# Output projections in three places: VectorE's order around the gates, and the sum of two gated branches moved from GpSimd to VectorE

## The reference

```python
# block one
y = sigmoid(g_a) * (o_a @ w_pa) + sigmoid(g_b) * (o_b @ w_pb)
out = y @ w_out
# each of the two layers
projected = einsum('bsnw,nwd->bsnd', branches, w_branch[l])     # three branches of width 512
merged = sum(gates * projected, axis=branch)
h = h + einsum('bsd,de->bse', merged, w_out[l])
```

## Time and profile before

| | us |
|---|---|
| median of 3 runs | 1981.39 (1981.3 to 1981.52) |
| the profiled execution, its own time | 1982.14 |
| its span in the trace | 1980.4 |
| TensorE busy | 1890.6 |
| VectorE busy | 1128.7 |
| GpSimd busy | 592.2 |
| ScalarE busy | 357.5 |

### The profile page before, as it was taken

The page is one execution under the profiler, slowest core; times in us unless marked ns, Lnnn a source line. Parts: engine busy times, 40 slices in busy tenths (PEclk is TensorE's granted clock), DMA queues, the critical chain, the costliest instruction groups (busy, mean ns, idle before and its releaser), DMA issues.

```text
span 1980.4 us, 32402 instructions
## 1 busy us (share of the span) xinstructions
PE 1890.6 (95%) x13598; PEld 1731.1 (87%) x13598; DVE 1128.7 (57%) x1178; ACT 357.5 (18%) x662; POOL 592.2 (30%) x507
## 2 busy tenths in 40 slices
PE   5999999999999988999989999899999999989999
PEld 2677777787999868999989998899999999889999
DVE  2743222335257976545476877765546687776554
ACT  2100000103121211211132123221112212322110
POOL 0111111211136303333433322433343332243433
PEclk8999999999999999999999999999999999999999
DMA  9235656321233514454534333344554433334552
GB/s 355 107 106 213 233 228 240 128 106 44 106 137 120 181 43 157 146 180 181 189 134 163 133 130 127 128 171 173 188 183 165 154 137 128 128 128 171 182 180 106
DMA packets 44910, 307.34 MB, mean 155 GB/s; under 512 B 5376, under 2 KB 5888, under 8 KB 8320
## 3 DMA queue, kind: packets, MB, share of 16 engines
q1 hardware_dynamic: 40912, 292.66, 40.9%
q10 hardware_dynamic: 3888, 13.03, 1.8%
HBM read 302.53 MB, written 3.15 MB: 154 GB/s over the span
## 4 chain that ended last, share of the span: by engine, by line
PE 85%; DVE 8%; POOL 3%; issue 2%; ACT 1%; DMA 1%; SPq 0%; ACTq 0%; DVEq 0%; POOLq 0%
PE ps L1838 25%; PE ps L1839 24%; PE ps L1840 24%; DVE wlo L686 2%; PE ps L1968 2%; POOL whi L613 2%; PE ps L2326 1%; DMA landing<-in_stream 1%; PE ps L1935 1%; PE ps L2227 1%; PE ps L2350 1%; PE ps L2336 1%; PE ps L2182 1%; DVE xlo L746 1%; PE ps L2299 1%
## 5 line engine op out<-in xcount | busy, mean ns | idle before, releaser
L1838 PE MATMUL ps<-xhi,whi 128*128 128x256 f32 (+1 forms) x3680 | 1120.5, 304 | 34.4 <-DVE xlo L694 17.7
L1839 PE MATMUL ps<-xlo,whi 128*128 128x256 f32 (+1 forms) x3680 | 1103.5, 300 | 0.0
L1840 PE MATMUL ps<-xhi,wlo 128*128 128x256 f32 (+1 forms) x3680 | 1103.0, 300 | 0.0
L686 DVE TENSOR_TENSOR wlo<-landing,whi 128x2048 fp32r<-128x2048 f32 x242 | 561.9, 2322 | 444.8 <-POOL whi L613 443.9
L1838 PEld LDWEIGHTS ps<-xhi,whi 128*128 128x128 f32 x3680 | 709.9, 193 | 69.8 <-issue 35.1
L1839 PEld LDWEIGHTS ps<-xlo,whi 128*128 128x128 f32 x3680 | 710.1, 193 | 22.4 <-issue 1.4
L1840 PEld LDWEIGHTS ps<-xhi,wlo 128*128 128x128 f32 x3680 | 709.7, 193 | 21.2
L612 POOL TENSOR_TENSOR whi<-landing,ones 128x128 fp32r<-128x128 f32 x242 | 131.3, 543 | 1370.0 <-PE ps L1840 1328.7
L613 POOL TENSOR_SCALAR whi<-landing 128x1920 fp32r<-128x1920 f32 x242 | 441.7, 1825 | 0.0
L1490 ACT ACTIVATE xhi<-big 128x512 fp32r (+3 forms) x66 | 45.9, 697 | 380.2 <-PE ps L1840 332.3
L909 DVE TENSOR_TENSOR big<-big,ps 128x512 f32<-128x512 f32 x22 | 15.1, 688 | 164.7 <-ACT big L1567 164.7
(11 more groups left out here) (258 smaller groups left out, 1254.8 us busy)
## 6 DMA issues: line engine op xcount, KB each, us to landing
landing<-in_stream SPq DMA_DIRECT2D x250, 1024.0 KB, 4.8
ws<-in_stream SPq DMA_DIRECT2D x28, 1024.0 KB, 5.4
spectra<-big ACTq DMA_DIRECT2D x8, 256.0 KB, 4.3
ws<-spectra ACTq DMA_DIRECT2D x2, 1024.0 KB, 4.9
ws<-in_tabs ACTq DMA_DIRECT2D x1, 1280.0 KB, 5.5
h<-in_xT ACTq DMA_DIRECT2D x1, 1024.0 KB, 6.1
ws<-in_ctxT ACTq DMA_DIRECT2D x1, 1024.0 KB, 15.2
ws<-in_window ACTq DMA_DIRECT2D x1, 1024.0 KB, 19.8
```

Source lines behind the costliest of these rows:

```text
L686: v.tensor_tensor(wlo[:, s % 2], landing[:, s], whi[:, s % 2].bitcast(F32), ALU.subtract).then_inc(lo_done, 1)
L1838: mm(out, w_hi, x_hi, start=first, stop=False, skip_group_check=True)
L1839: mm(out, w_hi, x_lo, start=False, stop=False, skip_group_check=True)
L1840: return mm(out, w_lo, x_hi, start=False, stop=last, skip_group_check=True)
```

## The change

GpSimd's two sums a layer go, and its panels run in the plain loop. VectorE does the same two sums (`two_sum`), the first ahead of the gate on bank 0 and the second ahead of the weights' low part of output panel 1. In the layers and in block one, the gate and the add of bank 0 now stand ahead of the weights' low part of panel 0, those of bank 1 behind `part_low` of panel 0, and those of banks 2 and 3 behind `part_low` of panel 1. The count of matmuls, of ScalarE's instructions and of DMAs stays.

```diff
--- before.py
+++ after.py
@@ -643,19 +643,6 @@
             whole = -(-end // UNROLL)
             for g in range(end, whole * UNROLL):
                 high(g, g % SLOTS, g // SLOTS)
-            for l in range(LAYERS):
-                behind = layer_panel(l, O_OUT)[0]
-                with pool.Fori(whole, behind // UNROLL) as i:
-                    for j in range(UNROLL):
-                        high(i * UNROLL + j, j, i)
-                whole = behind // UNROLL + 1
-                for g in range(behind - behind % UNROLL, whole * UNROLL):
-                    if g == behind:
-                        pool.wait_ge(gate_done, at(gate_done, l, 2))
-                    if 0 <= g - behind < 2:
-                        c = GT + 4 * (g - behind)
-                        pool.tensor_tensor(flatc(c, 4), flatc(c, 4), flatc(c + 8, 4), ALU.add).then_inc(gates_added, 1)
-                    high(g, g % SLOTS, g // SLOTS)
             with pool.Fori(whole, PANELS // UNROLL) as i:
                 for j in range(UNROLL):
                     high(i * UNROLL + j, j, i)
@@ -1096,17 +1083,35 @@
             for b in range(4):
                 last = v.tensor_tensor(flatc(MG + 2 * b, 2), flatc(MG + 2 * b, 2), ps[:, b], ALU.mult)
             last.then_inc(gate1_done, 1)
-            row_stage(G_PB, N_BR, chunk_src(ZC[0]), R_PB, R_PB, T, begun=True)
+            row_stage(G_PB, N_BR, chunk_src(ZC[0]), R_PB, R_PB, T, begun=True, last=False)
             dve.wait_ge(gate1_done, 1)
 
             def gated(b):
                 one, two = flatc(MG + 2 * b, 2), flatc(MG + 8 + 2 * b, 2)
+                if b < 3:
+                    dve.wait_ge(sums_out, 3 + b + 1)
+                else:
+                    dve.wait_ge(panel_used, G_PB + N_BR)
                 step(v.tensor_tensor(two, two, ps[:, 4 + b], ALU.mult))
                 v.tensor_tensor(one, one, two, ALU.add).then_inc(gate1_done, 1)
-                if b == 1:
-                    part_low(chunk_src(MG)(0), R_OUT1, R_OUT1, T)
-            residual(3, G_PB + N_BR, gated)
-            row_stage(G_OUT1, N_OUT, chunk_src(MG), R_OUT1, R_OUT1, T, begun=True)
+
+            def mixed_low(i):
+                low(G_OUT1 + i, (G_OUT1 + i) % SLOTS)
+
+            def mixed_part(i):
+                part_low(chunk_src(MG)(i), R_OUT1 + i, R_OUT1 + i, T)
+            gated(0)
+            mixed_low(0)
+            mixed_part(0)
+            gated(1)
+            mixed_low(1)
+            mixed_part(1)
+            gated(2)
+            gated(3)
+            for i in (2, 3):
+                mixed_low(i)
+                mixed_part(i)
+            mixed_low(N_OUT)
 
             def scaled_add(col, b0):
                 def add(b):
@@ -1321,18 +1326,49 @@
                 last.then_inc(gate_done, 1)
                 branch_low(2, 1)
                 branch_part(2, 1)
-                branch_low(2, 2)
+
+                def two_sum(n):
+                    if n == 0:
+                        dve.wait_ge(gate_done, at(gate_done, l, 2))
+                    c = GT + 4 * n
+                    v.tensor_tensor(flatc(c, 4), flatc(c, 4), flatc(c + 8, 4), ALU.add).then_inc(gates_added, 1)
 
                 def gated_last(b):
+                    if b < 3:
+                        dve.wait_ge(sums_out, at(sums_out, l, b + 1, base=12))
+                    else:
+                        dve.wait_ge(panel_used, branch_end(2))
                     lstep(gated(2, b))
-                    if b % 2 == 0:
-                        dve.wait_ge(gates_added, at(gates_added, l, b // 2 + 1))
+
+                def added_last(b):
+                    dve.wait_ge(gates_added, at(gates_added, l, b // 2 + 1))
                     v.tensor_tensor(flatc(GT + 2 * b, 2), flatc(GT + 2 * b, 2), flatc(GT + 16 + 2 * b, 2), ALU.add
                                     ).then_inc(gate_done, 1)
-                    if b == 1:
-                        part_low(chunk_src(GT)(0), rl + RO_OUT, R_LAYER + RO_OUT, T)
-                residual(at(sums_out, l, 0, base=12), branch_end(2), gated_last)
-                end = row_stage(layer_panel(l, O_OUT), N_OUT, chunk_src(GT), rl + RO_OUT, R_LAYER + RO_OUT, T, begun=True)
+
+                def out_low(i):
+                    low(layer_panel(l, O_OUT + i)[0], (G_LAYER + O_OUT + i) % SLOTS)
+
+                def out_part(i):
+                    part_low(chunk_src(GT)(i), rl + RO_OUT + i, R_LAYER + RO_OUT + i, T)
+                two_sum(0)
+                gated_last(0)
+                added_last(0)
+                out_low(0)
+                out_part(0)
+                gated_last(1)
+                added_last(1)
+                two_sum(1)
+                out_low(1)
+                out_part(1)
+                gated_last(2)
+                added_last(2)
+                gated_last(3)
+                added_last(3)
+                for i in (2, 3):
+                    out_low(i)
+                    out_part(i)
+                out_low(N_OUT)
+                end = layer_panel(l, O_OUT + N_OUT)[0]
 
                 def add_out(b, banks):
                     k = XHALVES[b][0]
```

## The result

The changed kernel takes 1964.16 us (median of 4 runs, 1963.42 to 1964.89) against 1981.35 (4 runs): ratio 0.9911, 95% interval 0.9898 to 0.9924. The forecast was 1962.3, the range 1957.0 to 1968.5. The profiled execution took 1964.7 us, its span is 1962.9; the span before was 1980.4.

The account below looks back on a forecast made before the run. TensorE, busy 95% of the span, was taken as the bound, with 17.7 us of waits on `xlo`. Gains of 7.0 us a layer (14.0) and 5.1 in block one, 19.1 together, gave a 1962.3 us median; range 1957.0 to 1968.5.

Parts of the forecast that it names:

- What holds `xlo` up: Layers: VectorE's `part_low` takes 2.85 us, not 0.69, beside GpSimd's sum; block one: the weights' low part goes first.
- the move of the sum: Layers: two GpSimd sums become VectorE sums of 1.23 us each; the 2.05 us wait before the last branch panel goes.
- The turn between half sum and rounding: Output panels: VectorE's half sum stands until GpSimd's rounding ends, or slips in between two GpSimd instructions.
- The value from the row: Block one, panel 2: bank 2's half sum slips between GpSimd's two instructions, as one did before in 0.56 us.
- the other case: If GpSimd always goes first, block one loses 0.9 us more at panel 2, the layers nothing.
- Low clock: Low-clock cost behind the longer waits goes: 2.2 us in each layer, 2.4 us in block one.
- Part of it is given back behind the stage: Rival: behind the stages a shifted clock phase costs 1.7 to 2 us per low stretch; 1966 or so, 0.14 with clock.
- the clock's: Rival: the new waits lower the clock in each stage, losing 6.8 us; 1969 us, chance 0.14 together with give-back.
- after it the order is the old one: Layers, behind output panel 3: VectorE's order is as before, so nothing further was added to the sum.
- The slower rival: Output panels: VectorE's queue becomes the bound, a layer costs 12.2 us against 9.6; 1991 us, chance 0.03.
- The Trainium skill's advice that a saturated VectorE may hand work to GpSimd: Layers: by that rule alone, the sums on VectorE would cost 2.4 us a layer, 4.9 us of the gain.
- the reading of the clock: Stages: waits under 2 us had not by themselves lowered the clock, so waits of 0.6 to 1.0 us should not.

Follow-up runs that it names:

- psum_half: Changed kernel with the last branch's gate product written back to its PSUM bank and read there by the half sum; 0.9882 of the kernel before, 1957.85 us.
- after_again: The changed kernel run once more, unaltered, beside later kernels; 1964.54 us, ratio 0.9914 to the kernel before.
- layers_only: Kernel before with only the layers' part of the diff, block one left as it was; 0.9934 of the kernel before, 1969.51 us.
- order_pool_sum: Changed kernel with the layers' two sums left on GpSimd, so the new order alone; 0.9936 of the kernel before, 1969.2 us.
- b1_only: Kernel before with only block one's part of the diff, layers left as they were; 0.9979 of the kernel before, 1977.36 us.

## Why the prediction was right

**What holds `xlo` up** and **the move of the sum**: as predicted. The forecast waits of 0.6, 0.8 and 1.0 us ahead of panels 0, 1 and 2 are 0.68, 0.75 and 0.91, as start minus slot (1264.43 - 1263.75, 1271.00 - 1270.25, 1277.74 - 1276.83), those of block one 0.27 and 0.65 are 0.32 and 0.66. Panel 1 of block one and panel 3 of both start in their slots, as walked. `psum_half` shows the reason that was only read from rows: two SBUF operands.

**The turn between half sum and rounding**: the half of bank 2 in block one did slip in between GpSimd's two instructions (0.96 us), and the rounding behind it took 2.26 us instead of 1.80. The value from the row held, and the 0.9 us of the other case did not come.

**Low clock**: 4.4 to 4.6 us in the layers and 2.4 in block one went, as summed. Measured at the stages: block one 5.1 us (5.18, less 0.10 that it was ahead before it), layer 0 7.15, layer 1 6.95, together 19.2 against 19.1 forecast. That agreement is no luck: each stage gains the same within 0.1 us in `after_again` (all three) and `layers_only` (the layers'), and no trace with waits under 1 us in a stage has a low stretch inside it.

**Part of it is given back behind the stage**: this rival came true in part and is the whole error of the profiled execution (1964.7 against 1963.0; the median is off by 1.9 us). It was held at 0.14 together with the clock's, with a term of 1.7 to 2 us, and was left out of the sum. What failed there is the step "after it the order is the old one": the order is, but the clock behind it is drawn anew. Outside the stages three low stretches differ. The new one from 788.0 costs 1.6 us. The new one from 1480.9 costs 0.9 and the one gone from 1303.7 gives 0.8, because waits behind a low stretch give part of it back; 0.1 us is lost behind layer 1's stage. Net 1.7 us: 1980.4 - 19.2 + 1.7 = 1962.9. So the term of 1.7 to 2 us for one stretch was at the upper end or above: they cost 0.8 to 1.6. That they came out as a loss of 1.7 us in this kernel and not as a gain was a draw.

**The slower rival** did not come: VectorE's queue is late by less than 1 us at every panel. **The Trainium skill's advice that a saturated VectorE may hand work to GpSimd** (Perfetto Trace Analysis, section Optimizing Scalar/DVE Operations) did not decide it: by `order_pool_sum` against the changed kernel, the sum on VectorE is worth 0.9936 - 0.9914, some 4 us, though the two intervals overlap a little; in the traces the layers' stages gain 6.7 us by it, and the wait of 1.89 us that goes with it is in the rows. The prediction gave half of that passage. It goes on that the two engines share an SBUF read port, so that moving work between them might not help, and the 2.85 us `part_low` beside GpSimd's sum agrees with that.

What was wrong without a cost is the reading of the clock, that waits under 2 us don't lower it. The clock fell behind a wait of 1.89 us in `b1_only` and one of 2.07 in `order_pool_sum`; and the trace of the kernel before already had it falling behind waits of 0.97 and 0.89 us that stand 1.8 us apart. That the waits of 0.5 to 0.8 us in the output panels, over 6 us apart, left it at 1.00 was expected and came.

## What to carry to other kernels

Where two engines exclude each other on operands in SBUF, count the one's instructions as time on the other's queue: a 4.3 us sum on an idle engine held up 0.7 us ones on the way to the matmuls. Walk the shared queue instruction by instruction and put each input just ahead of its own use; then look for an operand that can stay in PSUM, since here that took the exclusion away with no VectorE instruction getting longer. Sum a stage by its own waits, and widen the range by a low clock stretch or two up or down, 0.8 to 1.6 us each here: which ones appear changed with every shift of the kernel in time.

## What the runs showed of the hardware

- A VectorE `tensor_tensor` of 512 columns with one operand in PSUM takes 0.69 us beside a GpSimd rounding; with both in SBUF, where it met the rounding, it took up to 2.2 us (1.98 and 1.99 in layer 0), and ended 0.54 us behind GpSimd.
- A waiting VectorE instruction gets in between two GpSimd ones that follow each other (0.96 us, and GpSimd's next 2.26 instead of 1.80).
- The sum of 1024 columns takes 1.22 us on VectorE, 2.41 on GpSimd where VectorE is the one that stands, and 4.34 on GpSimd where it starts while VectorE's `low` is running (1258.54, `low` from 1258.38 to 1260.67).
- After the same wait of 1.89 us the clock stayed at 1.00 in the kernel before and fell to 0.57 in layer 0 of `b1_only`; behind the same pair of 0.97 and 0.89 us it fell in the kernel before and stayed at 1.00 in the changed one.
- `psum_half` writes a VectorE result back into the PSUM bank it read, at 0.68 to 0.70 us, the time of the write to SBUF.
